# A hybrid decoder trunk on one core: the rotary part of the attention scores in two products of stacked halves in place of three

## The chip, the cores and the metric

The kernel runs on one core of a Trainium2 chip. The metric is the device time of one execution in microseconds; the number reported is the median of a few executions. TensorE does the matrix products, ScalarE (ACT) and VectorE (DVE) work on rows of up to 128 partitions, GpSimd (POOL) does one elementwise job here, and the DMA queue of SyncE (SP) brings the weights in.

## The reference

A trunk of two layers serves a prompt of 256 tokens and 8 sample tokens (one each for 8 sequences with 1024 past tokens in a paged cache); all 264 tokens (T) go through together. Layer 0 is a gated token mixer and a feed-forward block, layer 1 multi-head latent attention (16 heads) and a feed-forward block. All of it is fp32. What the change touches is the score of the prompt's attention:

```python
q_nope, q_rope = q[..., :QK_NOPE_DIM], q[..., QK_NOPE_DIM:]   # 128 and 64 per head
q_rope = rope(q_rope, pos)
s = (jnp.einsum('bqhc,bkc->bhqk', qlb, c) + jnp.einsum('bqhr,bkr->bhqk', qrb, kr)) * ATTN_SCALE
s = jnp.where(kpos[None, :] <= qpos[:, None], s, -jnp.inf)
p = jax.nn.softmax(s, axis=-1)
```

The rotary key `kr` (64 wide) is one for all heads. The first term is a product over 128 or 256 dimensions per head, the second one over 64.

## The kernel before, in words

**Halves.** An fp32 operand x is kept as two fp32r tiles: hi, a copy rounded to fp32r by ScalarE, and lo = x - hi, made by VectorE (`lo_of`). A product of two such operands is three matmuls that add up in one PSUM tile, hi by hi, hi by lo and lo by hi (`passes`, L1311 to L1313); lo by lo is left out. The weights come as 222 slabs of 512 KB: DMA to `raw`, ScalarE to `whi` (`split`, L468), GpSimd to `wlo` (L397), in a ring of 4.

**The query stage.** It walks over 8 pairs of heads (p = 0 to 7). For a pair TensorE makes three query chunks of 9 matmuls each (`query_chunk(p, z)`): z = 0 holds the rotary parts of both heads on 64 rows each, z = 1 and 2 the plain parts. For z = 1 and 2 ScalarE writes `ohi` (L690, after an 8-column copy `qns`, L689) and VectorE `olo`. For z = 0 VectorE multiplies by sine and cosine (`query_rope`), TensorE swaps rows (`query_swap`, L1509) into bank 3 or 5, VectorE adds (`query_turned`, L1122), ScalarE writes the high half `qrhi` (`turned_queries`, L680), and VectorE the low half `qrlo` (`query_turned_low`). After the first two pairs this goes in groups of two pairs. In a group (g = 1, 2, 3) TensorE does two pairs of swaps, then the chunks of pairs 2g and 2g + 1. VectorE does, in this order: the two sums of the pairs before, `query_rope(2g)`, the two `qrlo`, for g = 1 the latents, and `olo` of pair 2g. ScalarE does the two `qrhi`, then slab splits and the `ohi` of pair 2g. A chunk with z = 1 of pair 2g + 1 waits on the semaphore `qlow_done` until `olo` of pair 2g, first head, has read its bank.

**The rotary key** has both of its halves of rows equal (its 64 columns are twice in the weight). It is kept in `krzhi` and `krzlo` as two versions, one for each head e of a pair: version e holds the key on the 64 rows of that head and zeros on the other 64 (four memsets, L1027 and L1028), so that a product over all 128 rows of `qrhi[:, p]` picks one head.

**The attention loop.** It walks over the same 8 pairs. For each pair TensorE runs `scores(p)`, `values(p)`, `turn(p, e)` (transposes of the probabilities, L1577), the keys of the next pair and `attend(p)`, with work for the 8 sample sequences in between (`sample_scores`, L1632 and L1636, `sample_attend`, L1656). VectorE takes the maximum (L1190) and normalises (L1201), ScalarE the exponentials (L729). In pair 6 the sample sequences are put together: VectorE makes their weights before its maxima of pair 6 (`weights`), and after these `selw` (`spread`, L1259), for which `sample_latents` (L1688) waits on TensorE. After the loop comes the output projection and the second feed-forward block.

Of the kernel before, what the change touches and what calls it, by code (L numbers as in the profile page):

```python
# [15 lines left out]
F32 = mybir.dt.float32  # L16
# [6 lines left out]
P = 128  # L23
# [65 lines left out]
def build(nc, xT, w_stream, w_uv, gains, v_gain, lat_gain, q_gain, wsT, ws00_in, bs, cosT, sinT, w_ukT, pages, table,  # L89
          y_out, c_out, kr_out, v_out):  # L90
    with ExitStack() as ctx:
# [75 lines left out]
        olo = sb("olo", [P, H, T], F32R)  # L167
        qrhi = sb("qrhi", [P, PAIRS, T], F32R)
        qrlo = sb("qrlo", [P, PAIRS, T], F32R)
        cT = sb("cT", [P, KL, T])  # L170
        kr = sb("kr", [P, T])
        cThi = sb("cThi", [P, KL, NP_], F32R)
        cTlo = sb("cTlo", [P, KL, NP_], F32R)
        krzhi = sb("krzhi", [P, 2, NP_], F32R)
        krzlo = sb("krzlo", [P, 2, NP_], F32R)
        pg = sb("pg", [P, BUFS, PAGES, PAGE])
# [36 lines left out]
        def room(p, n):  # L213
# [43 lines left out]

        swap_done, cqr_done, lat_done, cqs_done, cqhi_done, cqlo_done, krs_done, krsin_done, krswap_done, krsum_done, kr_done, krz_done, krhi_done, krlo_done = map(
            sem, ("swap_done", "cqr_done", "lat_done", "cqs_done", "cqhi_done", "cqlo_done", "krs_done", "krsin_done", "krswap_done", "krsum_done", "kr_done", "krz_done", "krhi_done",
                  "krlo_done"))  # L260
# [49 lines left out]
        def turned_bank(p):  # L310
            return ps[:, 5 if p % 2 else 3, 0:T]
# [149 lines left out]
        def _(act):  # L461
# [216 lines left out]
            def turned_queries(p):  # L678
                act.wait_ge(qr_done, p + 1)
                act.activation(qrhi[:, p, :], turned_bank(p), ACT.Copy).then_inc(qrhi_done, 1)  # L680

# [13 lines left out]
            act.wait_ge(krsum_done, 1)  # L695
            act.wait_ge(krz_done, 4)
            for e in range(2):
                act.activation(krzhi[64 * e:64 * e + 64, e, :], ps[64 * e:64 * e + 64, 5, 0:NP_],
                               ACT.Copy).then_inc(krhi_done, 1)
            act.activation(kr[:], ps[:, 5, 0:T], ACT.Copy).then_inc(kr_done, 1)  # L700
# [106 lines left out]
        def _(dve):  # L807
# [216 lines left out]
            s0, n0 = STAGES["dq"]  # L1024
            for e in range(2):
                other = slice(64 * (1 - e), 64 * (1 - e) + 64)
                dve.memset(krzhi[other, e, :].bitcast(F32), 0.0).then_inc(krz_done, 1)  # L1027
                dve.memset(krzlo[other, e, :].bitcast(F32), 0.0).then_inc(krz_done, 1)  # L1028
            dve.wait_ge(rope_in, 64)
# [53 lines left out]
            def keys_turned_low():  # L1083

                dve.wait_ge(krsum_done, 1)
                kr_ready(dve)
                for e in range(2):
                    dve.wait_ge(krhi_done, e + 1)
                    lo_of(krzlo[64 * e:64 * e + 64, e, :], ps[64 * e:64 * e + 64, 5, 0:NP_],
                          krzhi[64 * e:64 * e + 64, e, :]).then_inc(krlo_done, 1)  # L1090

# [32 lines left out]
            def query_turned_low(p):  # L1124

                dve.wait_ge(qrhi_done, p + 1)
                lo_of(qrlo[:, p, :], turned_bank(p), qrhi[:, p, :]).then_inc(qrlo_done, 1)

# [33 lines left out]
            def keys_low(p):  # L1162
# [4 lines left out]
            keys_low(0)  # L1167
            dve.wait_ge(qrlo_done, PAIRS)
            dve.tensor_tensor(qrs, qrhi[:, :, NP_:T].bitcast(F32), qrlo[:, :, NP_:T].bitcast(F32),
                              ALU.add).then_inc(qrs_done, 1)  # L1170
            dve.wait_ge(ql_done, 2)
            dve.tensor_copy(qlt[:, 2:4, :], key_views(7)).then_inc(qlb_done, 1)
            dve.wait_ge(qrs_done, 1)
            for z in range(2):
# [133 lines left out]
        def _(pe):  # L1308
# [190 lines left out]
            def query_swap(p):  # L1499

                pe.wait_ge(rope_sin, p + 1)
                if p == 0:
                    pe.wait_ge(psum_read, QA_N)
                elif p == 1:
                    pe.wait_ge(krlo_done, 2)
                    kr_ready(pe)
                else:
                    pe.wait_ge(qrlo_done, p - 1)
                pe.matmul(turned_bank(p), swap, tt[:, 1 + p % 2, :], start=True, stop=True).then_inc(rope_swap, 1)  # L1509
# [48 lines left out]
            def scores(p):  # L1558

                pe.wait_ge(klo_done, p + 1)  # L1560
                if p:
                    pe.wait_ge(ptlo_done, 2 * p)
                for e in range(2):
                    for lo, width, q0 in ((0, P, 0), (P, 2 * P, P)):
                        out = ps[:, 2 + e, lo:lo + width]
                        qs = slice(q0, q0 + P)
                        passes(out, ohi[:, 2 * p + e, qs], olo[:, 2 * p + e, qs], khi[:, e, 0:width], klo[:, e, 0:width],
                               True, False)
                        last = passes(out, qrhi[:, p, qs], qrlo[:, p, qs], krzhi[:, e, 0:width], krzlo[:, e, 0:width],
                                      False, True)  # L1570
                    last.then_inc(sc_done, 1)
# [157 lines left out]
            pe.wait_ge(qlow_done, 2 * PAIRS)  # L1729
            pe.wait_ge(qrlo_done, PAIRS)  # L1730
            pe.wait_ge(krlo_done, 2)
            for p in range(PAIRS):
# [135 lines left out]
```

## Time and profile before

| what | value |
| --- | --- |
| median of 3 runs | 753.21 us (752.96 to 753.37) |
| the profiled execution, its own time | 752.45 us |
| its span, first to last instruction | 750.7 us |
| TensorE busy (matmul) | 734.0 us, 98% of the span |
| GpSimd, ScalarE, VectorE busy | 538.9, 405.5, 295.9 us |
| granted TensorE clock, mean | 0.998 of full |
| chain that ended last | TensorE 82% of the span |
| HBM read | 142.42 MB, 192 GB/s over the span |

The profiled execution took 1.75 us more than its span; what lies around the span is no part of the trace. A matmul's row shows a modelled duration that overlaps with the next ones, so the pace of TensorE is read from the distance of start times, not from the durations.

### The profile page before, as it was taken

How to read it: one execution, taken by the hardware profiler on the slowest of the kernel's cores; microseconds unless marked ns; L12 is line 12 of the kernel's file. 1: busy time of each engine (PE TensorE's matmuls, PEld its weight loads, DVE VectorE, ACT ScalarE, POOL GpSimd, SP SyncE). 2: the span in 40 equal slices, each digit the busy share in tenths (PEclk: the TensorE clock that was granted, in tenths of full speed). 3: DMA queues.
4: the chain of work that ended last, by engine and by line, in shares of the span. 5: the costliest groups of instructions: out<-in, count | busy, mean ns of one | idle time of the engine just before them, and what ended most of it. 6: DMA issues, size and time to landing. Idle time of an engine off the chain costs nothing.

```text
span 750.7 us, 16856 instructions
## 1 busy us (share of the span) xinstructions
PE 734.0 (98%) x6315; PEld 715.7 (95%) x6315; DVE 295.9 (39%) x741; ACT 405.5 (54%) x725; POOL 538.9 (72%) x255
## 2 busy tenths in 40 slices
PE   6999999999999999999999999999999999999995
PEld 5999999999999999999999888789999999999995
DVE  5435855423323332232586655742233323331102
ACT  6867545455444444555675566554464444544542
POOL 7976675987888888888876121237868888788891
PEclk9999999999999999999999999999999999999999
DMA  8554453655767765565575798715546555555641
GB/s 313 193 185 141 137 173 109 207 190 189 258 227 222 237 193 190 188 202 200 172 268 169 239 291 280 259 49 178 176 158 203 194 168 180 184 186 182 204 157 59
DMA packets 44920, 144.66 MB, mean 193 GB/s; under 512 B 5602, under 2 KB 6882, under 8 KB 44610
## 3 DMA queue, kind: packets, MB, share of 16 engines
q1 hardware_dynamic: 44722, 143.53, 58.5%
q8 instruction: 35, 0.57, 0.3%
q0 software_dynamic: 144, 0.40, 0.1%
q14 instruction: 19, 0.16, 0.1%
HBM read 142.42 MB, written 1.48 MB: 192 GB/s over the span
## 4 chain that ended last, share of the span: by engine, by line
PE 82%; DVE 1%; ACT 0%; issue 0%; DVEq 0%
PE ps L1311 26%; PE ps L1312 25%; PE ps L1313 25%; PE ps L1656 1%; PE ps L1632 1%; PE ps L1577 1%; PE ps L1509 0%; PE ps L1636 0%; PE ps L1337 0%; PE ps L1713 0%; PE ps L1603 0%; PE ps L1646 0%; DVE h L1303 0%; PE ps L1688 0%; PE ps L1691 0%
## 5 line engine op out<-in xcount | busy, mean ns | idle before, releaser
L397 POOL TENSOR_TENSOR wlo<-raw,whi 128x1024 fp32r<-128x1024 f32 x222 | 529.0, 2404 | 192.1 <-ACT whi L468 191.8
L1311 PE MATMUL ps<-xhi,whi 128*128 128x264 f32 x1052 | 302.9, 288 | 0.2 <-POOL wlo L397 0.2
L1312 PE MATMUL ps<-xlo,whi 128*128 128x264 f32 x1052 | 298.4, 284 | 0.0
L1313 PE MATMUL ps<-xhi,wlo 128*128 128x264 f32 x1052 | 298.4, 284 | 0.0
L468 ACT ACTIVATE whi<-raw 128x1024 fp32r<-128x1024 f32 x222 | 233.9, 1055 | 55.4 <-PE ps L1313 53.5
L1311 PEld LDWEIGHTS ps<-xhi,whi 128*128 128x128 f32 x1052 | 198.6, 189 | 1.1 <-POOL wlo L397 0.4
L1312 PEld LDWEIGHTS ps<-xlo,whi 128*128 128x128 f32 x1052 | 198.8, 189 | 0.3
L1313 PEld LDWEIGHTS ps<-xhi,wlo 128*128 128x128 f32 x1052 | 197.8, 188 | 0.0
L1311 PE MATMUL ps<-ahi,whi 128*128 128x264 f32 x352 | 100.0, 284 | 0.0
L1313 PE MATMUL ps<-ahi,wlo 128*128 128x264 f32 x352 | 99.9, 284 | 0.0
L1312 PE MATMUL ps<-alo,whi 128*128 128x264 f32 x352 | 99.9, 284 | 0.0
L985 DVE TENSOR_TENSOR h<-ps,h 128x264 f32<-128x264 f32 x32 | 13.9, 433 | 153.5 <-PE ps L1313 153.5
L1313 PEld LDWEIGHTS ps<-ahi,wlo 128*128 128x128 f32 x352 | 66.3, 188 | 0.0
L1312 PEld LDWEIGHTS ps<-alo,whi 128*128 128x128 f32 x352 | 66.2, 188 | 0.0
L1311 PEld LDWEIGHTS ps<-ahi,whi 128*128 128x128 f32 x352 | 66.2, 188 | 0.0
L632 ACT ACTIVATE ahi<-ps 128x264 f32 (+1 forms) x44 | 17.2, 391 | 87.3 <-DVE ps L1004 87.3
L1001 DVE TENSOR_TENSOR ps<-ps,work 128x264 f32<-128x264 f32 x44 | 19.4, 442 | 104.4 <-PE ps L1313 104.4
L473 ACT ACTIVATE sq<-h 128x264 f32<-128x264 f32 x40 | 16.6, 423 | 57.7 <-DVE h L985 57.3
L629 ACT ACTIVATE sq<-ps 128x264 f32<-128x264 f32 x44 | 17.2, 390 | 41.2 <-DVE ps L999 41.2
L1311 PE MATMUL ps<-ghi,whi 128*128 128x264 f32 x128 | 36.6, 286 | 0.2 <-DVE glo L810 0.2
L1311 PE MATMUL ps<-ohi,whi 128*128 128x264 f32 x128 | 36.4, 284 | 0.0
L1312 PE MATMUL ps<-glo,whi 128*128 128x264 f32 x128 | 36.3, 283 | 0.0
(253 smaller groups left out, 1104.4 us busy)
## 6 DMA issues: line engine op xcount, KB each, us to landing
raw<-w_stream SPq DMA_DIRECT2D x222, 512.0 KB, 3.4
pg<-pages SPq DMA_DIRECT2D x64, 288.0 KB, 3.7
pg<-w_ukT SPq DMA_DIRECT2D x1, 2048.0 KB, 8.3
pg<-w_uv SPq DMA_DIRECT2D x1, 2048.0 KB, 10.8
h<-xT SPq DMA_DIRECT2D x4, 264.0 KB, 4.5
y_out<-h SPq DMA_DIRECT2D x4, 264.0 KB, 2.2
raw<-w_stream SPq DMA_DIRECT2D x2, 256.0 KB, 3.4
wsraw<-wsT SPq DMA_DIRECT2D x1, 512.0 KB, 7.2
```

What stands on the lines that cost most here:

```text
L397: pool.tensor_tensor(wlo[:, c % RING, :], raw[:, c % RING, :], whi[:, c % RING, :].bitcast(F32), ALU.subtract).then_inc(lo_ready, 1)
L468: act.activation(whi[:, c % RING, :], raw[:, c % RING, :], ACT.Copy).then_inc(hi_ready, 1)
L473: act.activation(sq[:, m % 2, :], src, ACT.Square).then_inc(sq_done, 1)
L629: act.activation(sq[:, w % 2, :], ps[:, (n0 + 2 * w) % BANKS, 0:T], ACT.Silu).then_inc(silu_done, 1)
L632: act.activation(ahi[:, i * 2 + w, :], ps[:, (n0 + 2 * w + 1) % BANKS, 0:T], ACT.Copy).then_inc(ahi_done, 1)
L985: dve.tensor_tensor(h[:, at, :], ps[:, (n0 + m) % BANKS, 0:T], h[:, at, :], ALU.add).then_inc(psum_read, 1)
L1001: dve.tensor_tensor(up, up, Ra[:], ALU.mult).then_inc(usc_done, 1)
L1311: pe.matmul(out, whi_, mhi, start=start, stop=False)
L1312: pe.matmul(out, whi_, mlo, start=False, stop=False)
L1313: return pe.matmul(out, wlo_, mhi, start=False, stop=stop)
L1577: last = pe.transpose(ps[:, 2 + e, b * P:b * P + P], pr[:, e, b * P:b * P + P], ident[:])
L1632: pe.matmul(strip(j), qsl[:, c, s, :], pg[:, b, 2 * j:2 * j + 2, c * P:(c + 1) * P], start=c == 0, stop=False)
```

## The change

The two heads of a pair no longer share one tile of high halves and one of low halves. Each head has a tile of its own, `qrb[:, head, 0:256]`, with the high half of its 64 rotary rows on its own 64 partitions and the low half on the other 64. The key is kept once, `krhi` and `krlo`, with the same 64 rows on both halves of the partitions. A product of `qrb` with `krhi` over 128 rows is then hi by hi plus lo by hi, and one with `krlo` is hi by lo plus lo by lo. The zeros and their memsets are gone. ScalarE writes the high half for each head apart (64 rows by 256 columns) and copies the 8 sample columns, unrounded, to `qrs`; VectorE writes the low half for each head apart, to the other 64 partitions; the sum `qrs = qrhi + qrlo` on VectorE (L1169) is gone.

```diff
-        qrhi = sb("qrhi", [P, PAIRS, T], F32R)
-        qrlo = sb("qrlo", [P, PAIRS, T], F32R)
+        qrb = sb("qrb", [P, H, NP_], F32R)
-        krzhi = sb("krzhi", [P, 2, NP_], F32R)
-        krzlo = sb("krzlo", [P, 2, NP_], F32R)
+        krhi = sb("krhi", [P, NP_], F32R)
+        krlo = sb("krlo", [P, NP_], F32R)
...
             def turned_queries(p):
                 act.wait_ge(qr_done, p + 1)
-                act.activation(qrhi[:, p, :], turned_bank(p), ACT.Copy).then_inc(qrhi_done, 1)
+                act.activation(qrs[:, p, :], turned_bank(p)[:, NP_:T], ACT.Copy).then_inc(qrs_done, 1)
+                for e in range(2):
+                    r = slice(64 * e, 64 * e + 64)
+                    act.activation(qrb[r, 2 * p + e, :], turned_bank(p)[r, 0:NP_], ACT.Copy).then_inc(qrhi_done, 1)
...
-            act.wait_ge(krz_done, 4)
-            for e in range(2):
-                act.activation(krzhi[64 * e:64 * e + 64, e, :], ps[64 * e:64 * e + 64, 5, 0:NP_],
-                               ACT.Copy).then_inc(krhi_done, 1)
+            act.activation(krhi[:], ps[:, 5, 0:NP_], ACT.Copy).then_inc(krhi_done, 1)
...
-            for e in range(2):
-                other = slice(64 * (1 - e), 64 * (1 - e) + 64)
-                dve.memset(krzhi[other, e, :].bitcast(F32), 0.0).then_inc(krz_done, 1)
-                dve.memset(krzlo[other, e, :].bitcast(F32), 0.0).then_inc(krz_done, 1)
...
-                for e in range(2):
-                    dve.wait_ge(krhi_done, e + 1)
-                    lo_of(krzlo[64 * e:64 * e + 64, e, :], ps[64 * e:64 * e + 64, 5, 0:NP_],
-                          krzhi[64 * e:64 * e + 64, e, :]).then_inc(krlo_done, 1)
+                dve.wait_ge(krhi_done, 1)
+                lo_of(krlo[:], ps[:, 5, 0:NP_], krhi[:]).then_inc(krlo_done, 1)
...
             def query_turned_low(p):
 
-                dve.wait_ge(qrhi_done, p + 1)
-                lo_of(qrlo[:, p, :], turned_bank(p), qrhi[:, p, :]).then_inc(qrlo_done, 1)
+                for e in range(2):
+                    dve.wait_ge(qrhi_done, 2 * p + e + 1)
+                    r, other = slice(64 * e, 64 * e + 64), slice(64 - 64 * e, 128 - 64 * e)
+                    lo_of(qrb[other, 2 * p + e, :], turned_bank(p)[r, 0:NP_], qrb[r, 2 * p + e, :]).then_inc(qrlo_done, 1)
...
-            dve.wait_ge(qrlo_done, PAIRS)
-            dve.tensor_tensor(qrs, qrhi[:, :, NP_:T].bitcast(F32), qrlo[:, :, NP_:T].bitcast(F32),
-                              ALU.add).then_inc(qrs_done, 1)
...
-                        last = passes(out, qrhi[:, p, qs], qrlo[:, p, qs], krzhi[:, e, 0:width], krzlo[:, e, 0:width],
-                                      False, True)
+                        pe.matmul(out, qrb[:, 2 * p + e, qs], krhi[:, 0:width], start=False, stop=False)
+                        last = pe.matmul(out, qrb[:, 2 * p + e, qs], krlo[:, 0:width], start=False, stop=True)
```

In the query stage two engines get other rows. On ScalarE, at the head of the first group (g = 1), there stands before:

```order
L680 ACTIVATE qrhi<-ps 128x264 [waits qr_done] x2
L468 ACTIVATE whi<-raw 128x1024 [waits slab_used,raw_ready3]
L689 ACTIVATE qns<-ps 128x8 [waits slab_used]
L690 ACTIVATE ohi<-ps 128x264
L468 ACTIVATE whi<-raw 128x1024 [waits slab_used,raw_ready0]
```

and now (`work` is the tile in which `qrs` lies):

```order
L679 ACTIVATE work<-ps 128x8 [waits qr_done]
L682 ACTIVATE qrb<-ps 64x256 x2
L679 ACTIVATE work<-ps 128x8 [waits qr_done]
L682 ACTIVATE qrb<-ps 64x256 x2
L467 ACTIVATE whi<-raw 128x1024 [waits slab_used,raw_ready3]
L691 ACTIVATE qns<-ps 128x8 [waits slab_used]
L692 ACTIVATE ohi<-ps 128x264
```

Two instructions have become six, ahead of the slab split and of `ohi`. On VectorE, in the same group, there stands before:

```order
L1111 TENSOR_TENSOR tt<-ps,work 128x264 [waits qr_done,rope_swap,q_done]
L1112 TENSOR_TENSOR sq<-ps,work 128x264
L810 TENSOR_TENSOR qrlo<-ps,qrhi 128x264 [waits qrhi_done] x2
L1096 SCALAR_TENSOR_TENSOR ps<-ps,gl,work 128x264 [waits rms_ready]
L1096 SCALAR_TENSOR_TENSOR ps<-ps,gl,work 128x264
L810 TENSOR_TENSOR olo<-ps,ohi 128x264 [waits qnhi_done] x2
```

and now:

```order
L1104 TENSOR_TENSOR tt<-ps,work 128x264 [waits qr_done,rope_swap,q_done]
L1105 TENSOR_TENSOR sq<-ps,work 128x264
L809 TENSOR_TENSOR qrb<-ps,qrb 64x256 [waits qrhi_done] x4
L1089 SCALAR_TENSOR_TENSOR ps<-ps,gl,work 128x264 [waits rms_ready]
L1089 SCALAR_TENSOR_TENSOR ps<-ps,gl,work 128x264
L809 TENSOR_TENSOR olo<-ps,ohi 128x264 [waits qnhi_done] x2
```

Two low halves have become four, ahead of the `olo` for which TensorE waits. On VectorE at the end of the query stage (`xlo` holds the low half of the keys of pair 0, `klo`), there stands before:

```order
L1122 TENSOR_TENSOR ps<-ps,sq 128x264 [waits rope_swap,rope_cos] x2
L810 TENSOR_TENSOR qrlo<-ps,qrhi 128x264 [waits qrhi_done] x2
L810 TENSOR_TENSOR xlo<-ps,xhi 128x512 [waits sc_done,khi_done]
L1169 TENSOR_TENSOR work<-qrhi,qrlo 128x64 [waits qrlo_done]
L1172 COPY work<-ps 128x512 [waits ql_done]
```

and now:

```order
L1115 TENSOR_TENSOR ps<-ps,sq 128x264 [waits rope_swap,rope_cos] x2
L809 TENSOR_TENSOR qrb<-ps,qrb 64x256 [waits qrhi_done] x4
L809 TENSOR_TENSOR xlo<-ps,xhi 128x512 [waits sc_done,khi_done]
L1164 COPY work<-ps 128x512 [waits ql_done]
```

The keys' low half, which the first scores wait for, stands behind four instructions in place of two, and the sum behind it is gone.

## Rows read from the trace of the kernel before

**Rows 1.** The page, part 1: busy time, share of the span, instructions.

```profile
PE 734.0 (98%) x6315; PEld 715.7 (95%) x6315; DVE 295.9 (39%) x741; ACT 405.5 (54%) x725; POOL 538.9 (72%) x255
```

**Rows 2.** Waits of TensorE, 380 to 502 us: us in total, times, longest.

```profile
PE ps L1311 <- DVE xlo L810: 0.9, 1, 0.9
PE ps L1688 <- DVE pg L1259: 0.2, 1, 0.2
```

**Rows 3.** Groups by form, TensorE: a product of the rotary scores.

```profile
L1312 PE MATMUL ps<-krzlo,qrhi 128*128 128x256 f32 x16 | 4.5, 281 | 0.0
```

**Rows 4.** Timeline of TensorE, pair 1, first head: start us, us, what.

```profile
424.90 0.28 PE L1312 MATMUL ps<-krzlo,qrhi 128*128 128x128 f32 x1
425.02 0.28 PE L1313 MATMUL ps<-krzhi,qrlo 128*128 128x128 f32 x1
...
425.65 0.28 PE L1312 MATMUL ps<-krzlo,qrhi 128*128 128x256 f32 x1
425.77 0.28 PE L1313 MATMUL ps<-krzhi,qrlo 128*128 128x256 f32 x1
```

**Rows 5.** Timelines of ScalarE and VectorE, then one line's instructions (L1176).

```profile
391.76 0.18 ACT L689 ACTIVATE qns<-ps 128x8 f32<-128x8 f32 x1 [0.22 <-PE ps L1313]
391.83 0.39 ACT L690 ACTIVATE ohi<-ps 128x264 fp32r<-128x264 f32 x1
...
382.64 0.78 ACT L698 ACTIVATE krzhi<-ps 64x256 fp32r<-64x256 f32 x2 [0.44 <-DVE ps L1081]
...
384.04 0.88 DVE L810 TENSOR_TENSOR krzlo<-ps,krzhi 64x256 fp32r<-64x256 f32 x2
...
L1176 DVE COPY qsr<-work x4: 203/220/223, 412.4 to 413.2; 64x64 f32<-64x64 f32 x4
```

**Rows 6.** Timelines, group 1 (g = 1); the last is chunk z = 1, pair 3.

```profile
387.31 0.65 ACT L680 ACTIVATE qrhi<-ps 128x264 fp32r<-128x264 f32 x2
...
388.10 0.76 DVE L810 TENSOR_TENSOR qrlo<-ps,qrhi 128x264 fp32r<-128x264 f32 x2
...
389.58 0.42 DVE L810 TENSOR_TENSOR olo<-ps,ohi 128x264 fp32r<-128x264 f32 x1
...
390.47 0.28 PE L1311 MATMUL ps<-xhi,whi 128*128 128x264 f32 x1
```

**Rows 7.** Timelines, group 3: `olo` of pair 6, chunk z = 1 of pair 7.

```profile
402.92 0.76 DVE L810 TENSOR_TENSOR qrlo<-ps,qrhi 128x264 fp32r<-128x264 f32 x2
403.80 0.43 DVE L810 TENSOR_TENSOR olo<-ps,ohi 128x264 fp32r<-128x264 f32 x1
...
405.28 0.28 PE L1311 MATMUL ps<-xhi,whi 128*128 128x264 f32 x1
```

**Rows 8.** Timelines, end of the query stage to the first scores.

```profile
408.96 0.73 ACT L680 ACTIVATE qrhi<-ps 128x264 fp32r<-128x264 f32 x2 [0.85 <-DVE ps L1122]
...
409.38 0.77 DVE L810 TENSOR_TENSOR qrlo<-ps,qrhi 128x264 fp32r<-128x264 f32 x2
...
409.96 0.60 ACT L719 ACTIVATE xhi<-ps 128x512 fp32r<-128x512 f32 x1 [0.27 <-PE ps L1313]
410.59 0.69 DVE L810 TENSOR_TENSOR xlo<-ps,xhi 128x512 fp32r<-128x512 f32 x1 [0.43 <-ACT xhi L719]
...
411.69 0.33 PE L1311 MATMUL ps<-xhi,ohi 128*128 128x128 f32 x1
```

**Rows 9.** Timelines, pair 6 of the attention loop.

```profile
484.66 0.28 DVE L1255 TENSOR_TENSOR pg<-on_diag,pg 8x128 f32<-8x128 f32 x1
484.87 0.27 DVE L1190 CUSTOM_DVE_ANT_0 tt<-ps,mask 128x128 f32<-128x128 f32 x1
...
486.94 0.62 PE L1688 MATMUL ps<-pg 8*16 8x256 f32 x8 [0.24 <-DVE pg L1259]
```

**Rows 10.** Timeline of GpSimd, from 396 us.

```profile
397.39 4.75 POOL L397 TENSOR_TENSOR wlo<-raw,whi 128x1024 fp32r<-128x1024 f32 x2 [0.25 <-ACT whi L468]
```

**Rows 11.** Timelines, pair 7: the last normalising and the turns behind it.

```profile
498.15 0.55 DVE L1201 TENSOR_SCALAR tt<-tt,rih 128x128 f32<-128x128 f32 x2
...
499.32 0.82 PE L1577 MATMUL ps<-ident,tt 128*128 128x128 f32 x6
```

More of the change, by code:

```diff
@@ L256, in build @@
         silu_done, act_done, ahi_done, alo_done = map(sem, ("silu_done", "act_done", "ahi_done", "alo_done"))
-        swap_done, cqr_done, lat_done, cqs_done, cqhi_done, cqlo_done, krs_done, krsin_done, krswap_done, krsum_done, kr_done, krz_done, krhi_done, krlo_done = map(
-            sem, ("swap_done", "cqr_done", "lat_done", "cqs_done", "cqhi_done", "cqlo_done", "krs_done", "krsin_done", "krswap_done", "krsum_done", "kr_done", "krz_done", "krhi_done",
+        swap_done, cqr_done, lat_done, cqs_done, cqhi_done, cqlo_done, krs_done, krsin_done, krswap_done, krsum_done, kr_done, krhi_done, krlo_done = map(
+            sem, ("swap_done", "cqr_done", "lat_done", "cqs_done", "cqhi_done", "cqlo_done", "krs_done", "krsin_done", "krswap_done", "krsum_done", "kr_done", "krhi_done",
                   "krlo_done"))
@@ L1167, in _ @@
             keys_low(0)
-            dve.wait_ge(qrlo_done, PAIRS)
-            dve.tensor_tensor(qrs, qrhi[:, :, NP_:T].bitcast(F32), qrlo[:, :, NP_:T].bitcast(F32),
-                              ALU.add).then_inc(qrs_done, 1)
             dve.wait_ge(ql_done, 2)
             dve.tensor_copy(qlt[:, 2:4, :], key_views(7)).then_inc(qlb_done, 1)
-            dve.wait_ge(qrs_done, 1)
+            dve.wait_ge(qrs_done, PAIRS)
             for z in range(2):
@@ L1504, in query_swap @@
                 elif p == 1:
-                    pe.wait_ge(krlo_done, 2)
+                    pe.wait_ge(krlo_done, 1)
                     kr_ready(pe)
                 else:
-                    pe.wait_ge(qrlo_done, p - 1)
+                    pe.wait_ge(qrlo_done, 2 * p - 2)
                 pe.matmul(turned_bank(p), swap, tt[:, 1 + p % 2, :], start=True, stop=True).then_inc(rope_swap, 1)
@@ L1729, in _ @@
             pe.wait_ge(qlow_done, 2 * PAIRS)
-            pe.wait_ge(qrlo_done, PAIRS)
-            pe.wait_ge(krlo_done, 2)
+            pe.wait_ge(qrlo_done, H)
+            pe.wait_ge(krlo_done, 1)
             for p in range(PAIRS):
```

## The prediction, made before the changed kernel ran

> **What bounds the kernel now.** I read the page's part 1 first: TensorE is busy for 98% of the span, and no other engine for more than 72% [rows 1]. Then the waits of TensorE in the stretch that the change touches, the query stage and the attention loop, 380 to 502 us: two waits, 0.9 us and 0.2 us, 1.1 us in 122 [rows 2]. So TensorE sets the end here, and work that is taken off it counts in full, unless a wait that is now covered comes to light. The question is then how much cover there is wherever ScalarE and VectorE get more to do, and wherever TensorE gets faster. For that I read the timelines: at what time the awaited instruction ends, and at what time TensorE first needs it. Below I call the difference the slack of that place. The clock has no part in it: the mean granted clock was 0.998 of the upper level, 2.4 GHz.
>
> **What TensorE loses.** Of three products of the rotary scores two are left. There are 8 pairs, 2 heads and 2 widths, so 32 matmuls go, 16 of them 256 columns wide [rows 3] and 16 of them 128. Their own duration of 281 ns is modelled and overlaps; the distance of starts is what one costs: 425.02 - 424.90 = 0.12 us with 128 columns, and 425.77 - 425.65 = 0.12 us with 256 [rows 4]; over the six products of a width in the same head the steps are 0.11 to 0.12. I take 0.114 on average, 32 x 0.114 = 3.65 us, bounds 3.5 and 3.8. Half the width saves nothing against the full width, so all 32 count alike. The products are over 128 rows before and after, and the weights are loaded for each product before and after, so the ones that stay cost what they did. Here a rule of the Trainium skill speaks for less. Its page "TensorE: Matmul & The Clock Gate", section "Back-to-back issue gap", gives about 81 ns for a matmul of 128 columns in a stream with weight loads; the trace has 0.11 to 0.12 us for it, so the trace disagrees and decides. By the page the 16 narrow ones would be worth 1.3 us and not 1.8, and the sum would be smaller by 0.5 us.
>
> **What ScalarE gets.** For each pair one copy of 128x264 becomes one of 128x8 and two of 64x256. The small one holds the next back by 391.83 - 391.76 = 0.07 us, and two of 64x256 took 0.78 us [rows 5], so a pair takes 0.07 + 0.78 = 0.85 us, and two pairs 1.7. Before, two pairs took 0.65 to 0.73 [rows 6, 8]. Two pairs are later by about 1.05 us. Half the rows save nothing.
>
> **What VectorE gets.** Two low halves of 64x256 took 0.88 us, of 128x264 0.76 us [rows 5, 6]. Four in place of two: 1.8 - 0.76 = about 1.04 us later for two pairs. The new ones write to the other half of the partitions. The nearest rows for this are the four copies of L1176, of which two cross and two don't: 203 to 223 ns, no difference to be seen [rows 5]. So one costs 0.45 us from start to start; the lower bound is the 0.38 of full-height ones (0.76 / 2), the upper one, if a crossing write costs half as much again, 0.68.
>
> **Where the two meet TensorE.** (a) Group 1. `olo` of pair 2 ends at 389.58 + 0.42 = 390.00, and the chunk that waits for it starts at 390.47 [rows 6]: slack 0.47. On VectorE it now comes 1.04 later, on ScalarE its `ohi` 1.05 to 1.1 later. Stall: 1.05 - 0.47 = 0.6 us. The next chunk waits for `olo` of the other head, which is as late, and by then TensorE is as late too: nothing more. (b) Groups 2 and 3 have no latents ahead of `olo`. In group 3 it ends at 404.23 and is needed at 405.28 [rows 7]: slack 1.05, lateness 1.0 to 1.1. Group 2 reads within 0.02 us the same. Stall 0 to 0.1 each, I take 0.1 for both. (c) The end of the query stage. ScalarE starts at 408.96 and now ends its six copies at 410.66; `khi` (L719), which began at 409.96, begins then, 0.7 later, and `klo` ends at 411.98 in place of 411.28. VectorE's four low halves end at 409.38 + 1.8 = 411.18, which is earlier, so ScalarE is the later one. The first scores started at 411.69 [rows 8]: slack 0.41. Stall: 0.3 us. (d) The slabs. The splits on ScalarE come up to 1.1 us later. The GpSimd instructions from 397.39 have the second of their two low halves done at 402.14 [rows 10], and this slab is not needed before the end of the query stage, over 5 us later; the slabs before it stand likewise. Nothing. The DMA issues of SP that follow GpSimd's progress move by the same 1.1 us and have room too. (e) The removed memsets, the second key copy and its low half, and the sum L1169 lie on VectorE and ScalarE where TensorE doesn't wait: nothing, except that 0.2 us of VectorE time ahead of the first maxima make up for part of (c). I don't count it.
>
> **Where TensorE's gain is lost in the loop.** The chain from scores to maximum, exponential, normalising and turn starts with the end of the scores, so it moves along with them. The tightest pair is 7, where the last normalising ends at 498.70 and the turns start at 499.32 [rows 11]; that distance stays. But in pair 6 something starts elsewhere. VectorE comes out of the sample weights at 484.87 and goes straight into the maxima, without idle time, and then to `selw`, for which TensorE waits 0.24 us at 486.94 [rows 9]. That chain began before the scores of pair 6, so TensorE can't come to `sample_latents` earlier than 486.94, however short these scores are. The saving of pair 6, 4 x 0.114 = 0.46 us, turns into a longer wait there.
>
> **The sum.** -3.65 + 0.6 + 0.1 + 0.3 + 0.46 = -2.2 us. The profiled execution took 752.45 us and would take 750.25. The median of the three runs, 753.21, lies 0.76 above it, so for the median I say 751.0 us. A difference of about 0.2% (1.5 us) is what a measurement of this kernel can tell from no change.
>
> **Rivals.** (1) *The cover is better than I read.* If the half-height instructions follow each other at the pace of the full ones, 0.38 on VectorE and 0.34 on ScalarE, group 1 stalls 0.25, the end 0.1 and the others nothing: gain 3.65 - 0.35 - 0.46 = 2.8, time 750.4, at best 749.9. For it: only one pair of half-height instructions of each engine is in the trace. (2) *Little is left.* The query stage has four places of which each is late by four low halves. Let s be the us from start to start of such an instruction. Group 1 stalls for 4s - 0.76 - 0.47. Groups 2 and 3 stall for 4s - 1.95 each (the `olo` of 403.80 ends at 402.92 + 4s + 0.43, with 402.92 the start of the low halves before it, and 405.28 is when it is needed). The end stalls for 4s - 1.6 (409.38 + 4s against 410.59, less the slack of 0.41). A negative one counts as zero. At s = 0.55 they add up to 2.1 us, and the gain is 1.1: 752.1. The same comes out if two more pairs of the loop lose their 0.46 us as pair 6 does. Against it are the krzlo pair and L1176 [rows 5]. (3) *Slower: a low half that crosses to the other partitions goes in two passes.* Then s is twice 0.42, 0.84 us; the query stage is bound by VectorE, the stalls are 2.1 + 2.8 + 1.8 = 6.7 us, and with pair 6 the kernel is 3.5 us slower: 756.7. It is slower than the bound of 1.5 us from s = 0.71 on. Nothing in the trace shows a crossing write with two inputs; the crossing copies speak against it. (4) *The change doesn't do what it says.* The order of the changed kernel has 32 matmuls fewer and nothing else on TensorE, so this gets no chance.
>
> **Chances.** Forecast 0.46 (gain 1.5 to 2.6), rival 1 0.26, rival 2 0.20, rival 3 0.08. Faster by over 0.2%: forecast and rival 1, 0.72. Within 0.2%: rival 2, 0.20. Slower: 0.08. The range takes in rival 1 to its best end, with 0.1 us for the spread of the runs, and rival 2 down to a gain of 0.7: 749.8 to 752.5 us.
>
> **What the profile after would show.** TensorE has 32 matmuls fewer in the scores, and a pair's scores last 2.3 us in place of 2.8. Among its waits there are new ones: about 0.6 us on `olo` before the chunk z = 1 of pair 3, about 0.3 us before the first scores, on `klo`, and the wait at L1688 grows from 0.24 to about 0.7. On VectorE a low half of 64x256 to the other partitions takes 0.42 us, and four of them 1.8. If the first wait is missing, rival 1 is right; if there are waits of this kind in groups 2 and 3 of more than 0.1 us, look at the duration of these instructions (rivals 2 and 3). I would be wrong altogether if TensorE's pace in the query chunks or in the scores changed, which no row suggests.

## The result, and the profile after

| what | before | after |
| --- | --- | --- |
| median (lowest to highest, executions) | 753.0 us (752.75 to 753.66, 10) | 754.28 us (752.43 to 756.07, 10) |
| ratio, 95% interval | | 1.0016 [1.0009, 1.0024] |
| the profiled execution, its own time | 752.45 us | 756.07 us |
| its span | 750.7 us | 753.6 us |

The changed kernel is not faster: 1.3 us slower in the median, 2.9 us longer in the profiled span. It lies 3.3 us above the predicted 751.0 and outside the range. Its ten executions spread over 3.6 us, those of before over 0.9. The profiled execution of after is the slowest of its ten (three have its span of 753.6 us, six have 750.7 to 751.8), so what follows prices each loss as it stands in a long execution.

Part of the difference lies outside the span. In every execution of before that was taken beside the experiments, and in every one of the experiments in which TensorE has as many products as before (e2, e4, e5, e7, e12), the time is 1.6 to 1.9 us longer than the span; in after it is 1.7 to 3.4 us longer, 2.3 in the median, and the other kernels with fewer products have such executions too. The median span of after is 751.7 us, that of before 751.3 to 751.4. So 0.3 to 0.4 of the 1.3 us are in the span. The trace ends with the span and doesn't show what the rest is; sums of terms from a trace are therefore compared with spans below.

The page of after, part 1, shows that the matmuls that were to go are gone, 6283 in place of 6315 [rows 1]:

```profile
PE 732.5 (97%) x6283; PEld 712.0 (94%) x6283; DVE 298.4 (40%) x743; ACT 408.8 (54%) x740; POOL 539.3 (72%) x255
```

TensorE is busy 1.5 us less and the span is 2.9 us longer, so it waits 4.4 us more. The waits of TensorE in the profile of after say where (us in total, times, longest; the 7.6 at the start of the kernel was 7.2 before and is left out):

```profile
PE ps L1624 <- DMA pg<-pages: 2.4, 1, 2.4
PE ps L1303 <- DVE xlo L809: 1.3, 2, 0.9
PE ps L1303 <- DVE olo L809: 0.7, 1, 0.7
...
PE ps L1680 <- DVE pg L1251: 0.5, 1, 0.5
...
PE ps L1669 <- DVE pg L1243: 0.2, 1, 0.2
```

Three of these the prediction named: `olo` in group 1, `klo` ahead of the first scores (0.4 of the 1.3; the other 0.9 stands in [rows 2] too), and `selw` in pair 6 (L1680, 0.24 before [rows 9]). The largest it did not: at L1624 TensorE waits 2.4 us for a page of the cache. This is `sample_scores(6)`, the scores of sample sequence 6 in pair 4. The timeline of TensorE there, after:

```profile
462.75 1.06 PE L1648 MATMUL ps<-pg,sq 128*16 128x256 f32 x16
466.23 1.91 PE L1624 MATMUL ps<-pg,qsl 128*16 128x256 f32 x16 [2.42 <-DMA pg<-pages]
467.91 1.08 PE L1628 MATMUL ps<-pg,qsr 128*16 128x128 f32 x16
468.92 0.76 PE L1569 MATMUL ps<-ident,tt 128*128 128x128 f32 x3
469.43 0.36 PE L1303 MATMUL ps<-cThi,whi 128*128 128x256 f32 x1
```

And the same instructions before:

```profile
463.02 1.06 PE L1656 MATMUL ps<-pg,sq 128*16 128x256 f32 x16
463.90 1.05 PE L1632 MATMUL ps<-pg,qsl 128*16 128x256 f32 x16
464.76 0.62 PE L1636 MATMUL ps<-pg,qsr 128*16 128x128 f32 x16
465.31 0.55 PE L1577 MATMUL ps<-ident,tt 128*128 128x128 f32 x3
465.61 0.36 PE L1311 MATMUL ps<-cThi,whi 128*128 128x256 f32 x1
```

TensorE could have begun at 466.23 - 2.42 = 463.81 at the latest, about when it did before: by then the five pairs of shorter scores had paid for the later query stage. The 2.42 us count from the modelled end of the instructions ahead. By start times the loss is larger: L1624 follows L1648 by 466.23 - 462.75 = 3.48 us, before it was 463.90 - 463.02 = 0.88, so 2.6 us are lost here. Behind the wait there is a second loss. From L1624 to the first product of the keys, after takes 469.43 - 466.23 = 3.20 us, before 465.61 - 463.90 = 1.71. The table of stretches has the reason (us, then busy time of each engine, then the granted clock, DMA share and GB/s). After:

```profile
463.00:466.00 3.00, 0.81 (x16) 0.22 (x8) 1.31 (x4) 0.97 (x4) 0.00 (x0) 1.00 0.89 275
466.00:469.00 3.00, 2.77 (x33) 1.25 (x34) 0.00 (x0) 0.00 (x0) 0.00 (x0) 0.50 0.92 280
469.00:472.00 3.00, 3.00 (x25) 3.00 (x26) 1.54 (x3) 1.98 (x6) 0.00 (x0) 0.93 0.84 244
```

The granted clock is 0.50 for the three us behind the wait, the level of 1.2 GHz, after TensorE had stood idle for 2.42 us; in the same stretches of before it is 1.00. That costs 3.20 - 1.71 = 1.5 us. (In e9, below, the same instructions stand behind a shorter wait with the clock at 1.00 and take 465.29 - 463.56 = 1.73 us, so it is the clock and not the wait that stretches them.)

The page comes late because of SyncE. These are its issues of page loads in this stretch, before (a page is 288 KB of the cache, 8 pages are a sample sequence; the weight slabs between them are left out):

```profile
412.54 7.98 SPq L349 DMA_DIRECT2D pg<-pages  x8
...
423.94 17.11 SPq L349 DMA_DIRECT2D pg<-pages  x16
...
442.29 7.95 SPq L349 DMA_DIRECT2D pg<-pages  x8
...
451.47 17.87 SPq L349 DMA_DIRECT2D pg<-pages  x16
```

And after:

```profile
414.12 7.97 SPq L348 DMA_DIRECT2D pg<-pages  x8
...
425.52 17.99 SPq L348 DMA_DIRECT2D pg<-pages  x16
...
444.74 8.31 SPq L348 DMA_DIRECT2D pg<-pages  x8
...
454.28 17.80 SPq L348 DMA_DIRECT2D pg<-pages  x16
```

From the pages of sample 3 on SP goes on almost without a pause: about 1.1 us a page (17.11 / 16), with one weight slab after the pages of samples 4 and 5. It starts sample 2 when the query stage is over and sample 3 when the first sample sequence is attended to, so it starts 1.6 us later in both, and it is 2.8 us later at the last row. The chain of waits of after runs over it (the pieces in order of time: start us, us, what; L347 is the read of the page's number from the table, L348 the issue):

```profile
461.61 0.33 SPq L348
461.98 0.27 SPq L347
462.28 0.15 SPq L347
462.69 3.50 DMA pg<-pages
466.23 1.91 PE ps L1624 x16
```

The eighth page of sample 6 was issued at 462.69 and landed 3.50 us later, at 466.19. In before this part of the chain holds nothing but TensorE, but the instructions of the tile `pages` between 460 and 461 us have its eighth page (last two lines of that answer):

```profile
L349 SPq DMA_DIRECT2D pg<-pages x1: 333/333/333, 460.1 to 460.1; - x1
...
DMA to landing us min/median/max: 3.3/3.3/3.3
```

It landed at 460.1 + 3.3 = 463.4, and TensorE took it at 463.90. The slack was 0.5 us, in a place where there was no wait, so no row of waits spoke of it. After, the page landed 2.8 us later and TensorE came 0.1 earlier: 2.8 + 0.1 - 0.5 = 2.4, the wait of the profile (2.6 by start times, by which TensorE would have come 0.27 earlier).

**The balance of the profiled execution.** TensorE begins the first scores at 413.75 against 411.69, +2.06. Of this, 0.28 us were there before the change can act: the swaps of group 1 start at 385.52 against 385.24, and this offset differs from trace to trace (385.17 in e6, 386.19 in e5). The 32 matmuls give -3.65, the page wait +2.6, the clock +1.5, L1680 and L1669 +0.3 and +0.15. The sum is +2.95. The products of L1705 in pair 7 (L1713 before) start at 498.87 against 495.94, +2.9, and the span is 2.9 longer.

### The profile page after: what moved, and what is told of

It reads as the page before. It is cut to its first block, busy times and chain, and to the rows that moved or that the text cites. A ratio compares the mean times of both kernels' runs of the same rounds, so it can differ in the third digit from the quotient of the medians.

```text
span 753.6 us, 16808 instructions
## 1 busy us (share of the span) xinstructions
PE 732.5 (97%) x6283; PEld 712.0 (94%) x6283; DVE 298.4 (40%) x743; ACT 408.8 (54%) x740; POOL 539.3 (72%) x255
## 4 chain that ended last, share of the span: by engine, by line
PE 74%; SPq 4%; DVE 2%; issue 2%; ACT 1%; DMA 0%; DVEq 0%
PE ps L1303 24%; PE ps L1304 23%; PE ps L1305 23%; SPq L348 2%; SPq L347 2%; PE ps L1624 1%; DMA pg<-pages 0%; PE ps L1569 0%; PE ps L1501 0%; PE ps L1329 0%; PE ps L1648 0%; PE ps L1705 0%; DVE pg L1225 0%; PE ps L1628 0%; DVE qrb L809 0%
```

## The experiments

Two theories stood against each other at first: that the new low and high halves cost more than their stalls show (the query stage), and that the gain goes to the page loads of SP, which don't get faster with TensorE. A result is given as the median (lowest to highest, number of executions), then the ratio to the kernel before on the same chip, whose medians were 753.08 to 753.16 us, with its 95% interval.

**One part alone: the products (e1).** Before, with lo by hi of the rotary scores left out; the query stage is untouched.

```diff
-                        last = passes(out, qrhi[:, p, qs], qrlo[:, p, qs], krzhi[:, e, 0:width], krzlo[:, e, 0:width],
-                                      False, True)
+                        pe.matmul(out, qrhi[:, p, qs], krzhi[:, e, 0:width], start=False, stop=False)
+                        last = pe.matmul(out, qrhi[:, p, qs], krzlo[:, e, 0:width], start=False, stop=True)
```

> The kernel before with two of the three rotary products (the low half of the queries by the high half of the key is left out), nothing else changed: the query stage costs what it did. Queue theory (SP issues the page loads one after the other, and the last page of sample 6 arrives just when TensorE needs it): TensorE gets to sample_scores(6) about 4 x 0.46 = 1.8 us earlier and waits there for a page by 1.5 to 2 us, perhaps with a lower granted clock behind it (up to 1.6 us); with pair 6's 0.46 lost the total is 753.0 - 3.65 + 0.46 + 1.7 = 751.5, up to 753.1 with the clock. Rival (only the query stage and pair 6 cost anything): no page wait, 749.8.

Measured: 751.57 us (750.6 to 753.56, 11), 0.9983 [0.9974, 0.9992]. That is -1.6 us, as expected from a page wait, and half of what 32 matmuls less the loss in pair 6 should give (3.2). The timeline of TensorE:

```profile
463.22 1.06 PE L1632 MATMUL ps<-pg,qsl 128*16 128x256 f32 x16 [1.25 <-DMA pg<-pages]
```

With the query stage as before, SP is about as early as before (451.79 against 451.47), TensorE would be there at 463.22 - 1.25 = 461.97, 1.9 us earlier, and the slack is 0.5: 1.9 - 0.5 = 1.4, and 1.25 was measured; the page landed at about 463.2, 0.2 earlier than before. The faster loop runs into the page by itself. The clock stays at 1.00 behind this shorter wait.

**The other part alone: the halves (e2).** After, with a third product added to each score, so that TensorE does what it did before (the scores are not right then).

```diff
                         pe.matmul(out, qrb[:, 2 * p + e, qs], krhi[:, 0:width], start=False, stop=False)
+                        pe.matmul(out, qrb[:, 2 * p + e, qs], krlo[:, 0:width], start=False, stop=False)
                         last = pe.matmul(out, qrb[:, 2 * p + e, qs], krlo[:, 0:width], start=False, stop=True)
```

> The changed kernel with a third product put back in each score (a second one with the low half of the key, so the values are not right): TensorE has as many matmuls as before, and only the query stage is new. Both theories: the stalls of the query stage, 1.3 to 1.9 us, so 754.3 to 754.9. Queue theory in particular: no page wait, since SP's page loads and TensorE's loop start later together and TensorE is no faster. If instead the page wait is there, the late start of the loads alone is its cause.

Measured: 754.88 us (754.7 to 755.76, 8), 1.0025 [1.0014, 1.0035], +1.7 us. No page wait: TensorE and SP are late by the same. So the halves cost 1.7 us, where the prediction had 1.0. In spans it is the same, 753.1 against 751.4.

**Two slab loads behind the pages of samples 6 and 7,** in after (e3) and, as a control, in before (e4).

```diff
-                if s in (4, 5):
-                    load(PR_S + 3 + s)
+                if s in (6, 7):
+                    load(PR_S + 1 + s)
```

> The changed kernel with two weight-slab loads on SP moved from behind the pages of samples 4 and 5 to behind those of 6 and 7. Queue theory: each takes SP 1.2 us between page loads, so the last page of sample 6 lands 2.3 us earlier, the page wait of 2.4 us and the lower clock behind it (1.6 us) go, and the time falls by 2 to 4 us to 750.5 to 752. Rival: no change from 754.3.

> The kernel before with the same move of the two slab loads. Queue theory: TensorE waits for no page before, so nothing to gain: within 0.3 us of 753.0. If it is faster by more, the kernel before already had page waits in some executions.

Measured: after 753.53 us (752.24 to 755.95, 11), 1.001 [1.0, 1.002]; before 752.99 (752.6 to 753.99, 11), 1.0 [0.9991, 1.0009]. In the profile the page wait has shrunk from 2.4 to 1.3 us and the clock stays at 1.00 behind it. This is half of the 2.3 us that I expected, and the time is above the 750.5 to 752 that I had forecast: each slab took one page's time on the queue, but the pages themselves come no faster:

```profile
425.49 36.15 SPq L348 DMA_DIRECT2D pg<-pages  x32
```

That is 1.13 us a page. The median of the changed kernel is 0.8 us lower than without the move, but the two intervals overlap, so I take only the shorter wait from this run; before gains nothing.

**The queue made slower, in before (e5).** Three spare reads of the table behind the pages of sample 3.

```diff
+                if s == 3:
+                    for g in range(3):
+                        sp.value_load(tab[0:1, g:g + 1], min_val=0, max_val=PHYS - 1)
```

> The kernel before, with three spare table reads on SP behind the page loads of sample 3 (0.5 to 0.7 us each), so that the pages of samples 4 to 6 are issued 1.5 to 2 us later; TensorE's work is untouched. If the kernel before has no slack for its pages, TensorE waits for sample 6 by 1 to 2 us, perhaps with the lower clock behind it: 754 to 756.5. If the pages had slack (rival: the page wait of the changed kernel comes from something else in it), 753.2. If not the issue on SP but the bytes bind, the delay is partly made up: 753.5 to 754.

Measured: 754.01 us (753.41 to 755.0, 11), 1.001 [1.0001, 1.0019], +0.9 us. Nothing on TensorE, ScalarE, VectorE or GpSimd was changed, and a page wait appears in a kernel that had none:

```profile
465.37 1.06 PE L1635 MATMUL ps<-pg,qsl 128*16 128x256 f32 x16 [0.34 <-DMA pg<-pages]
```

The group with the reads took 18.73 us in place of 17.11, and the next one won back 1.2. So before stands close to this wait, as its slack of 0.5 us says. I had expected a wait of 1 to 2 us and 754 to 756.5, so the effect is at the low end. The profiled wait is smaller than the loss in the median; I count this run for the sign, not for the size.

**The pages made faster, in after (e6) and in before (e7).** The page's number is a constant, so the read of the table falls away. The sample sequences then attend to other pages of the cache, so their output isn't the reference's; all loads and products keep their sizes, but the addresses change too.

```diff
-                at = sp.value_load(tab[0:1, s * PAGES + g:s * PAGES + g + 1], min_val=0, max_val=PHYS - 1)
+                at = s * PAGES + g
```

> The changed kernel with page numbers written into the program in place of the table's (the sample values are then not the reference's): SP reads no table, so a page costs it 0.4 to 0.7 us in place of 1.1. If SP's serial issue binds, the pages of sample 6 are there long before, no page wait, and what is left is the query stage (+1.7), pair 6 (+0.46) and the saving (-3.65): 751.5. If the DMA's bytes bind, the page wait stays at 1 to 2.5 us: 753 to 754.5.

> The kernel before with the page numbers written into the program, the control for the one ahead: TensorE waited for no page, so 753.0 by every theory, within 0.3.

Measured: after 752.1 us (751.44 to 753.12, 11), 0.9985 [0.9976, 0.9994]; before 753.16 (752.66 to 753.55, 11), 1.0 [0.9991, 1.0009]. Before doesn't care; after loses its page wait and 2.2 us. Its issues:

```profile
413.04 4.33 SPq L348 DMA_DIRECT2D pg<-pages  x8
```

That is 0.54 us a page in place of 1.0 to 1.1. (That other addresses alone made the transfers faster is not ruled out by this pair; the run with a second queue, below, keeps the table's pages and reaches 387 GB/s.) Its waits of TensorE between 384 and 510 us are the ones that the prediction named, and no other:

```profile
PE ps L1303 <- DVE xlo L809: 1.3, 2, 0.9
PE ps L1303 <- DVE olo L809: 0.7, 1, 0.7
PE ps L1680 <- DVE pg L1251: 0.5, 1, 0.5
```

This pair separates the two theories: with the pages out of the way the change is worth -1.06 us of time (752.1 against 753.16), with them +1.3. In median spans it is 749.9 against 751.4, -1.5 us, and with them +0.3 to +0.4.

**The query stage put in another order (e9).** In after, on ScalarE and VectorE, the halves of a group's second pair stand behind `ohi` and `olo` of the next pair, at the end behind `khi` and `klo`; TensorE waits for the last pair's halves only before pair 7.

```diff
...
                 query_turned_low(2 * g - 2)
-                query_turned_low(2 * g - 1)
-                if g == 1:
-                    latents()
                 query_low(2 * g, 0)
+                if g == 1:
+                    latents()
                 query_low(2 * g, 1)
                 query_rope(2 * g + 1)
+                query_turned_low(2 * g - 1)
...
```

> The changed kernel with another order in the query stage: on ScalarE and VectorE the rotary halves of the second pair of a group come behind the plain halves of the next pair's heads, and those of pair 7 behind the keys of pair 0. The stalls of the query stage (0.95, 0.16, 0.17 and 0.4 us by the profile) should fall to 0.3 in all, so the loop and the page loads start 1.3 us earlier, and as the pages bind until sample 6, all of it moves: 754.2 - 1.3 = 752.9. If the query stage were not where that time went, no change.

Measured: 752.36 us (751.23 to 754.47, 11), 0.9996 [0.9987, 1.0005]: 1.9 us better than after, and no difference to before that could be told. All new waits of the query stage are gone (the swaps start at 385.40, 392.87, 400.40 and 407.81, so a group lasts 7.41 to 7.53 us, before 7.40 to 7.41), and the page wait stays:

```profile
463.56 1.06 PE L1624 MATMUL ps<-pg,qsl 128*16 128x256 f32 x16 [1.42 <-DMA pg<-pages]
```

Removing the stalls that were predicted does not bring the predicted gain; the page is next.

**Sample 6 taken later (e8),** in after, at the end of pair 4 in place of its middle (the table says which sample sequence goes with which pair):

```diff
-        MID = (0, 2, 3, 4, 6, 7, None, None)
-        END = (1, None, None, 5, None, None, None, None)
+        MID = (0, 2, 3, 4, None, 7, None, None)
+        END = (1, None, None, 5, 6, None, None, None)
```

> The changed kernel with the scores of sample 6 moved from the middle of pair 4 to its end (MID and END tables), some 4 us later on TensorE, and nothing else. If the wait for the pages of sample 6 is what takes the gain: that wait goes; but then TensorE comes to sample 7 in pair 5 at about 473 us, with its last page issued at 472 and landing 3.5 us later, so a wait of 1 to 2 us stands there. Together 752.5 to 753.5. If the place of sample 6 didn't matter: 754.2.

Measured: 752.96 us (751.96 to 753.88, 11), 0.9999 [0.999, 1.0008]. The wait moves on to the next sample sequence:

```profile
467.76 1.06 PE L1624 MATMUL ps<-pg,qsl 128*16 128x256 f32 x16
475.27 1.06 PE L1624 MATMUL ps<-pg,qsl 128*16 128x256 f32 x16 [0.91 <-DMA pg<-pages]
```

**Three edits together (e10):** query order, sample 6 later, slabs later.

> The changed kernel with three moves: the order in the query stage (as in the run on that), sample 6 later, and the two slab loads behind the pages of 6 and 7. No query stalls, page wait for sample 6 gone, at sample 7 0 to 1.5 us. 753.1 - 3.65 + 0.46 + 0.2 = 750.1 with no page wait, up to 751.6 with one. If it is not below the 752.4 of the query order alone, the page loads are not what is left.

Measured: 751.75 us (750.53 to 754.9, 11), 0.9986 [0.9977, 0.9996]. This is just above the 751.6 that I had as the upper bound. A wait of 0.46 us for sample 7's pages is left: the queue is as long as before, whatever the order in which its pages are used.

**Some pages on a second queue (e11, and e12 in before).** In e11, after with the query order above, three of the eight pages of samples 3 to 7 are read and issued by GpSimd, which is idle most of the loop; in e12, as a control, the same in before without the query order.

```diff
...
-                for g in range(PAGES):
+                for g in range(PAGES if s < 3 else PAGES - 3):
                     load_page(s, g)
...
+            for s in range(3, NS):
+                pool.wait_ge(spv_done, s - 2)
+                for g in range(PAGES - 3, PAGES):
+                    at = pool.value_load(tab[0:1, s * PAGES + g:s * PAGES + g + 1], min_val=0, max_val=PHYS - 1)
+                    pool.dma_start(pg[:, s % BUFS, g, :], pages[at]).then_inc(pages_pool[s % BUFS], 16)
+                if s > 3:
+                    splits(PR_S + s, PR_S + s + 1)
...
```

> The changed kernel with the new order of the query stage, and 3 of the 8 pages of each sample from the fourth on issued by GpSimd (idle for 80% of the attention loop) in place of SP: SP's chain falls from 1.1 us x 8 to 1.1 us x 5 per sample. Queue theory: no page wait, all that is left is pair 6: 753.1 - 3.65 + 0.46 + 0.2 = 750.1. If the DMA's bytes bind, 751.5 to 752.5 as with the query order alone.

> The kernel before with the same share of pages on GpSimd, the control: TensorE waited for no page, so 753.1 within 0.3; slower only if GpSimd's issues delay its slabs.

Measured: after 750.97 us (749.62 to 752.0, 9), 0.9968 [0.9958, 0.9978], the best of all; before 753.26 (752.73 to 754.19, 11), 1.0002 [0.9993, 1.0011]. After is 0.9 us above the 750.1 that I had expected. No page wait is left; in pair 6 the 0.5 and 0.2 us stay:

```profile
425.35 11.57 SPq L349 DMA_DIRECT2D pg<-pages  x10
...
463.46 1.05 PE L1635 MATMUL ps<-pg,qsl 128*16 128x256 f32 x16
```

Against its control the change with the query order is worth 2.3 us of time, and 2.9 us of span (medians 748.6 and 751.5). The prediction's terms without its query stalls make 3.65 - 0.46 = 3.2. Against the query order alone (752.36) the second queue brings 1.4 us; before gains nothing from it. The query order was not run in before; the one wait of before in the query stage, 0.9 us [rows 2], stands in e9 too.

## Why the prediction was wrong

- **What TensorE loses (-3.65): right.** 32 matmuls went, and the narrow and the wide ones step by 0.11 to 0.12 as they did [rows 4]. The trace of e1 up to sample 6 agrees: L1656, the last instructions ahead of sample 6, starts there at 460.91 against 463.02, and that trace is 0.21 us later from the query stage on (swaps at 385.45 against 385.24), so 20 matmuls fewer gave 2.11 + 0.21 = 2.3, and 20 x 0.114 is 2.3.
- **The price of a half-height instruction: right; that of the full-height ones that it replaces was read too high.** I took 0.45 us from start to start on VectorE and 0.85 for a pair's three copies on ScalarE [rows 5]. After has, on each engine in group 1:

```profile
388.51 1.78 DVE L809 TENSOR_TENSOR qrb<-ps,qrb 64x256 fp32r<-64x256 f32 x4
...
387.60 0.16 ACT L679 ACTIVATE work<-ps 128x8 f32<-128x8 f32 x1
387.66 0.77 ACT L682 ACTIVATE qrb<-ps 64x256 fp32r<-64x256 f32 x2
388.46 0.18 ACT L679 ACTIVATE work<-ps 128x8 f32<-128x8 f32 x1
```

  Four low halves in 1.78, three copies in 0.86. Writing to the other partitions costs nothing (two low halves of 64x256 that didn't cross took 0.88 before [rows 5]), so rivals 1 and 3 are out, and rival 2 with its s = 0.55 too. What was mis-sized is what they replace. I took 0.76 us for two full-height low halves, from the first start to the last end. But full-height instructions overlap with the next one, and the instruction behind these two started 0.68 us after the first:

```profile
388.78 0.89 DVE L1096 SCALAR_TENSOR_TENSOR ps<-ps,gl,work 128x264 f32<-128x264 f32 x2
```

  The same instruction after starts at 390.32, 390.32 - 388.51 = 1.81 us behind the first of four. The difference is 1.13 us and not 1.04. (Rival 1 has a slip too: its formula gives 0.29 for group 1, and 0.25 was written. Nothing rests on it.)
- **The query stage (+1.0): the right places, too small.** The group lasted 392.64 - 385.24 = 7.40 us before and 393.88 - 385.52 = 8.36 after, +0.96 where I had 0.6; the others +0.16 and +0.18 where I had 0.1 for both. The end shows a wait of 0.40 where I had 0.3:

```profile
413.75 0.30 PE L1303 MATMUL ps<-xhi,ohi 128*128 128x128 f32 x1 [0.40 <-DVE xlo L809]
```

  Together 1.7, as e2 measured. In group 1 the low halves begin 0.13 us later after the swaps than before (388.51 - 385.52 against 388.10 - 385.24), four of them and the latents take 1.15 us more and not 1.04, and TensorE starts 0.05 after the end of what it waits for (391.61 against 391.56). The 0.13 has the same reason as the 1.15: before, the first low half started while the instruction ahead of it was still running (388.10, and L1112 runs from 387.76 to 388.18), after, it starts behind that one's end. My slack had also been read to the end of `olo` with no allowance for the 0.05. A tenth or two at each place make 0.7 us of error in all.
- **Pair 6 (+0.46): right.** L1680 waits 0.53 in place of 0.24, and L1669 ahead of it 0.15 that it hadn't.
- **The DMA issues of SP: the step that failed.** In (d) the prediction had it that "the DMA issues of SP that follow GpSimd's progress move by the same 1.1 us and have room too". It looked at the slabs alone, and the sum has no term for the page loads: they were put at nothing without a row. No rival has them either; the second form of rival 2, that more pairs of the loop lose their saving, comes nearest. The pages of samples 2 to 7 follow TensorE's progress: the end of the query stage starts them, and a queue that is then busy until 469 us almost without a pause sets when they land. It had 0.5 us of slack at sample 6, less than the 2.3 that I expected the loop to gain up to there (20 x 0.114). So "TensorE sets the end here, and work that is taken off it counts in full, unless a wait that is now covered comes to light" was the right sentence, and I looked for such waits on ScalarE and VectorE alone. The wait costs 2.4 us in the profile (2.6 by start times), and e6 shows 2.2 for the page wait with the clock in the median times, 1.8 in the median spans.
- **"The clock has no part in it": wrong,** but only as a result of the wait. It doubled the price of it in the profiled execution.
- **The signs.** With the pages out of the way the sum is -3.65 + 1.7 + 0.46 = -1.5, and e6 against e7 gives -1.5 in median spans, -1.06 in median times. The page wait with its clock turns it to +0.3 to +0.4 in spans, +1.3 in times. The query stage's delay moves TensorE and the queue alike, and so does the saving of pair 0, since the pages of sample 3 start behind it. What turns into the page wait, whatever the query stage does, is the saving of pairs 1 to 4 less the slack: 16 x 0.114 - 0.5 = 1.3 us. e1 and e9 show that part alone (1.25 and 1.42). The rest of the 2.4 us is the queue's own lateness: from the pages of sample 3 to the last row it took 454.28 - 425.52 = 28.76 us, before 451.47 - 423.94 = 27.53.

What stays open is why single page issues take 0.7 to 1.25 us in place of 0.33 (SP at 433.51 and 457.93 in the chain of after; before has such ones too, 0.97 us at 457.3): with them the queue of after fell another 1.2 us behind, on top of the 1.6 of its start. No run separates them from the rest of the traffic. Open is also what the executions spend outside the span, up to 1.7 us more with fewer products.

## What to carry to other kernels

No wait in the profile does not mean slack: before work is taken off the bound engine, follow each transfer that it consumes back from landing to issue, and add up the queue's issues from the point that starts it. A chain of issues that runs without a pause beside the bound engine is a second bound, and it has to be shortened or split over two queues at the same time as the engine; alone, either edit is worth nothing or less. When instructions are added ahead of one that the bound engine waits for, put them behind it where the data allow it, rather than trust a slack of a few tenths.

## What the runs showed of the hardware

- **The clock behind a wait.** After an idle time of 2.42 us of TensorE the granted clock was 0.50 for three us, and it cost 1.5 us (one trace). After 1.25 (e1), 1.30 (e3) and 1.42 us (e9) at the same place it stayed 1.00. All executions list their span and mean clock: in e9 eight have 749.4 to 750.4 us at 0.996 to 0.998 and three 751.9 to 752.2 at 0.995, with nothing between; in e3 eight have up to 751.9 and three 753.1 to 754.0 at 0.995 or 0.996; in the kernels without a page wait (e2, e6, e7, e11, e12) none is below 0.996, but neither is one in e1, e5 and e8, which have a page wait, and e10 has one execution at 0.995 with a wait of 0.46 us in its trace. So the same code with a page wait seems to fall into the lower clock in some executions and not in others, a step of about 2 us. It is read from the means, not from traces of those executions, and with the time outside the span it would account for the wide spread of after.
- **A page issue with a number read from a table** costs SP 1.0 to 1.1 us from start to start, with a fixed address 0.54 in the first eight of e6. GpSimd took 0.55 us for the issue and about as much between two (e11).
- **DMA had room.** With faster issues the core's DMA moved 374 to 420 GB/s between 460 and 469 us (e6), against 260 to 274 before, and 387 GB/s at 463 to 466 us in e11, with the table's pages on two queues, so it was the issuing and not the transfers that set the pace. That is about all the room there was: in e6 the DMA share rose from 0.85 to 0.87 before to 1.01 to 1.09, and the median time of a page from issue to landing from 3.4 us before to 4.9 (e6) and 5.3 (e11). In e6:

```profile
466.00:469.00 3.00, 3.00 (x35) 2.73 (x36) 1.57 (x3) 2.69 (x7) 0.12 (x1) 1.00 1.01 420
```

- **Half the partitions, more than the whole price.** Copies and low halves of 64 rows by 256 columns, alternately on the lower and the upper half, follow each other at 0.40 us on ScalarE and 0.45 on VectorE, a little more than one lasts alone (0.36 to 0.38 and 0.42): nothing of two such instructions overlaps. Full-height ones of 264 columns last as long alone (0.37 and 0.42), but the next starts after 0.28 and 0.34 us. No run shows whether the height or the change of partitions takes the overlap away.
